# Two-layer decoder with a mixture of experts: the first expert's weight slot handed back in two halves, and the first two experts written out ahead of TensorE's loop

## The chip, the cores and the metric

The kernel runs on one core of a Trainium2 chip, in one launch. The metric is device time in microseconds (us), the median of several runs. Unless it says otherwise, a number with a decimal point below is in us.

## What is computed

A trunk of two layers over 256 tokens of width 1024, all in float32. Layer 0 mixes tokens by a causal convolution module, layer 1 by sparse attention. Each layer then runs a mixture of 32 experts and a gated embedding. The part that matters here, cut down:

```python
def hier_moe(xn, w_rg, b_rg, w_re, b_re, w_gate, w_up, w_down):
    ...                                 # router: top group, then its top 2 experts for each token
    def expert_block(args):
        xblk, e = args
        h = jax.nn.silu(xblk @ w_gate[e]) * (xblk @ w_up[e])    # w_gate, w_up: 1024 x 512
        return h @ w_down[e]                                    # w_down: 512 x 1024
    yb = lax.map(expert_block, (xb, blk_e)).reshape(P, D)
    out = jnp.zeros((N, D), yb.dtype).at[slot_tok].add(yb * slot_w[:, None].astype(yb.dtype))
    return out.reshape(B, T, D)
```

Each token goes to 2 of 32 experts, so an expert sees 16 tokens on average; its three matrices have 2 MB each, 6 MB in all.

## The kernel before, in words

Every engine has a program of its own, and semaphores order them. In both layers all 32 experts are computed, one after the other, each on a slot of 32 tokens. An expert whose tokens don't fit takes extra rounds: they stand in a conditional block ahead of its ordinary code (`pe.If(more > 0)` in `one_expert`, line 671), which holds a second copy of all of the expert's matmuls and is jumped over when there is nothing extra.

**TensorE** (`moe`, `one_expert`). An ordinary expert is, in this order: `gate_up` (line 589), the product of the gathered tokens with gate and up, 32 calls that run over the contraction in 8 steps k = 0 to 7; the gather of the tokens of the expert after it (L580); the transposes of h (L601); the product with down (L608); the transposes of the next tokens (L586); and the scatter into the sums in PSUM (L615). `gate_up` ends with an increment of `gu_mm`, the product with down with one of `y_mm`. The 32 experts are a loop of 16 rounds (line 722) with the code of two experts in it, one for each of the two buffers.

**Weights.** The tile `ring` has two buffers. Each holds gate, up and down of one expert, 48 KB in each of 128 partitions. Even experts use buffer 0 (its three thirds are `R0[0]`, `R0[1]` and `R0[2]`), odd experts buffer 1. The elements of a partition lie in the order of k, so the first 2048 of gate or of up are k = 0 to 3.

**The queue of loads.** All weights are loaded by SyncE's queue (SP), in the order in which its program issues them; a wait in that program holds back all that stands behind it. `expert` (line 320) waits until `gate_up` of the expert two before is done (`gu_mm`), issues gate and up, waits for that expert's product with down (`y_mm`), and issues down. `experts` (line 337) orders a layer: experts 0 and 1 have been loaded before it begins. It first loads the gate of expert 19 in two pieces of 1 MB into tiles that have come free: the first piece into `xnT` once the router's product is done (L345), the second into `h` once ScalarE has copied `h` to the sums (L347, L348). Then comes a loop over pairs of experts from expert 2 on. Parts of experts 16, 17 and 18 are held in other tiles too and are left out of the loop's loads (`held`).

So in the order of the queue: second piece of expert 19's gate; gate and up of expert 2 (wait for `gu_mm` of expert 0); down of expert 2 (wait for `y_mm` of expert 0); gate and up of expert 3 (wait for `gu_mm` of expert 1); and so on.

Of the kernel before, what the change touches and what calls it, by code (L numbers as in the profile page):

```python
# [36 lines left out]
NG, NE, NEG_E = 4, 32, 8  # L37
# [37 lines left out]
def build(nc, x, p, positions, g_mix, g_ffn, g_ple, conv_w_pw1, conv_b_pw1, conv_w_dw, conv_b_dw,  # L75
# [3 lines left out]
    with ExitStack() as ctx:  # L79
# [3 lines left out]
        def sem(name):  # L83
            return ctx.enter_context(nc.semaphore(name))
# [53 lines left out]
        xgT = carve(256).rearrange("p (k s) -> p k s", k=8)  # L138
# [92 lines left out]
        def dense(buf):  # L231
# [3 lines left out]
        R0 = [ring[:, 0, 4096 * i:4096 * (i + 1)] for i in range(3)]  # L235
# [35 lines left out]
        in_in = [sem(f"in_in{i}") for i in range(5)]  # L271
        gu_in = [sem(f"gu_in{i}") for i in range(2)]
        held_in = sem("held_in")
        dn_in = [sem(f"dn_in{i}") for i in range(2)]
        out_st = sem("out_st")
        c_pool, c_dve, c_act = sem("c_pool"), sem("c_dve"), sem("c_act")
# [14 lines left out]
        gu_mm, sil_ok, h_ok, ht_mm, hT_ok, y_mm, y_ok = [  # L291
            sem(s) for s in ("gu_mm", "sil_ok", "h_ok", "ht_mm", "hT_ok", "y_mm", "y_ok")]
# [24 lines left out]
        def _(sp):  # L317
# [20 lines left out]
            def experts(L):  # L338
                def pair(it, held=(None, None)):
                    for s in range(2):  # L340
                        expert(L, it * 2 + s, s, it * 2 + (s - 1 + NE * L), held[s])
                m = HELD // 2
                spare = moe_w_gate[L, HELD + 3].rearrange("(p k) f -> p (k f)", k=8)
                sp.wait_ge(rt_mm, L + 1)
                sp.dma_start(HX[0], spare[:, 0:2048]).then_inc(held_in, 16)  # L345
                sp.wait_ge(hn_dve, HN_AT[3 * L + 1])
                sp.wait_ge(acc_ok, 4 * (L + 1))  # L347
                sp.dma_start(HX[1], spare[:, 2048:4096]).then_inc(held_in, 16)  # L348
                with sp.Fori(1, m) as it:
                    pair(it)  # L350
                pair(m, (0, 1))
                pair(m + 1, (2, 0))
                if L == 0:
                    sp.wait_ge(pp_ok, 4)
                    for i, v in enumerate((nsa_q_norm[0:1, :], nsa_k_norm[0, 1:2, :], nsa_k_norm[0, 2:3, :], nsa_k_norm[0, 0:1, :])):
                        sp.dma_start(gn[:, i, :], v.broadcast_to([P, DH])).then_inc(rot_in, 16)
                    sp.dma_start(invb, inv_freq.broadcast_to([P, DH // 2])).then_inc(rot_in, 16)
                with sp.Fori(m + 2, NE // 2) as it:
                    pair(it)
                for n in range(2):  # L360
                    sp.dma_start(dense(WB[n]), cols(ple_w_gate[L], n)).then_inc(ple_in[n], 16)
# [8 lines left out]
            for i, (c0, c1) in enumerate(PW1_PARTS):  # L370
                for g in range(2):
                    w = conv_w_pw1[0].rearrange("(k p) n -> p k n", p=P)[:, :, D * g + P * c0:D * g + P * c1]
# [68 lines left out]
        def _(pe):  # L441
# [80 lines left out]
            for c in range(KD):  # L522
# [6 lines left out]
                for g in range(2):  # L529
                    w = dense(PW1[2 * (c // 4) + g])  # L530
                    for k in range(KD):
                        xnT_ready(0, k, 1)
                        i = pe.matmul(PS[:, c % 4, g * T:(g + 1) * T], w[:, k, (c % 4) * P:(c % 4 + 1) * P],
                                      xnT[:, k, :], start=(k == 0), stop=(k == KD - 1))
# [51 lines left out]
                    i = pe.transpose(PS[:, BGX, Q4 + P * c:Q4 + P * (c + 1)], xg[:, c::2], ident[:, :])  # L586
                return i

            def gate_up(s, xT):
                for k in range(8):  # L590
                    for j in range(4):
                        w = w_gu(s)[:, j // 2, :, :]
                        i = pe.matmul(PS[32 * j:32 * j + 32, BGU, 0:256].rearrange("q (p c) -> q p c", c=2), xT[:, k, :],  # L593
                                      w[:, k, :].rearrange("q (p h c) -> q h p c", h=2, c=2)[:, j % 2],
                                      start=(k == 0), stop=(k == 7))
                return i

            def h_T():
# [20 lines left out]
            def moe(L):  # L619
# [48 lines left out]
                xg_T().then_inc(xt_mm, 1)  # L668
                rows(W4, 7).then_inc(rt_row, 1)

                def one_expert(it, s):
                    n = it * 2 + (s + NE * L + 1)
                    gi = it * 2 + (s + g0 + 2)
                    ld = it * 16 + 16 * (NE // 2 * L + 1)
                    e = it * 2 + s
                    pe.wait_ge(tab_ok, L + 1)
                    more = pe.value_load(tab[0:1, 0, bass.ds(e, 1)], min_val=0, max_val=7)

                    with pe.If(more > 0):
                        before = pe.value_load(tab[0:1, 1, bass.ds(e, 1)], min_val=0, max_val=64)  # L680
                        pe.wait_ge(xgT_ok, gi - 1)
                        pe.wait_ge(row_act, L + 1)
                        pe.wait_ge(row_dve, L + 1)
                        pe.wait_ge(acc_ok, 4 * (L + 1))
                        pe.sem_inc(pe_step, 1)
                        with pe.Fori(0, more) as r:
                            c = before + r + 1
                            pe.wait_ge(X["x_sel"], c)
                            gather(xsel).then_inc(X["x_ga"], 1)
                            pe.wait_ge(X["x_xg"], c)  # L690
                            xg_T().then_inc(X["x_xt"], 1)
                            pe.wait_ge(X["x_xgT"], c)
                            pe.wait_ge(gu_in[s], ld * 2)
                            gate_up(s, xxgT).then_inc(X["x_gu"], 1)
                            pe.wait_ge(X["x_h"], c)
                            h_T().then_inc(X["x_ht"], 1)
                            pe.wait_ge(X["x_hT"], c)
                            pe.wait_ge(dn_in[s], ld)
                            down(s).then_inc(X["x_y"], 1)
                            pe.wait_ge(X["x_wT"], c)  # L700
                            pe.wait_ge(X["x_ysb"], c)
                            scatter(xwT).then_inc(X["x_done"], 1)

                    pe.wait_ge(gu_in[s], ld * 2)
                    pe.wait_ge(xgT_ok, gi - 1)
                    gate_up(s, xgT).then_inc(gu_mm, 1)
                    pe.wait_ge(sel_ok, it * 2 + (s + (NE + 2) * L + 2))
                    gather(sel[1 - s]).then_inc(ga_mm, 1)
                    pe.wait_ge(row_dve, L + 1)
                    pe.wait_ge(h_ok, n)  # L710
                    h_T().then_inc(ht_mm, 1)
                    pe.wait_ge(row_act, L + 1)
                    pe.wait_ge(dn_in[s], ld)
                    pe.wait_ge(hT_ok, n)
                    down(s).then_inc(y_mm, 1)
                    pe.wait_ge(xg_ok, gi)
                    xg_T().then_inc(xt_mm, 1)
                    pe.wait_ge(wT_ok, gi - 1)
                    pe.wait_ge(y_ok, n)
                    pe.wait_ge(acc_ok, 4 * (L + 1))  # L720
                    scatter(wT[s]).then_inc(wT_free, 1)
                with pe.Fori(0, NE // 2) as it:
                    one_expert(it, 0)
                    one_expert(it, 1)

# [1157 lines left out]
```

## Time and profile before

| | us |
|---|---|
| median of 3 runs (lowest, highest) | 1302.53 (1300.98, 1304.65) |
| the profiled execution, its own time | 1307.97 |
| its span, first to last instruction | 1305.9 |
| TensorE busy in matmuls | 1035.2 (79%) |
| TensorE busy loading weights | 586.6 (45%) |
| VectorE, ScalarE, GpSimd busy | 320.3, 300.4, 456.9 |
| mean granted clock of TensorE | 0.904 of full speed |
| read from HBM | 447.70 MB |

Busy times of different engines overlap. A row of the timeline gives the start, the length, the engine, the line of the code, the operation, the tiles and the count of merged instructions; in brackets stands how long the engine was idle before it and what ended that. "issue" there means that the profile shows nothing that the engine waited for. PEclk is the granted clock of TensorE: 1.00 is 2.4 GHz, 0.50 is 1.2 GHz. L593 is the matmul in `gate_up`; a call of it shows as two matmul records and two weight loads, so one expert's `gate_up` is 64 matmuls. q1 is the queue of the weights, q8 carries instructions, in packets of 16 KB.

### The profile page before, as it was taken

What the parts mean: (1) busy time and instruction counts of PE and PEld (TensorE: products, weight loads), DVE (VectorE), ACT (ScalarE), POOL (GpSimd) and SP (SyncE); (2) the same over time, 40 slices, a digit from 0 to 9 for tenths busy, and PEclk for the clock granted to TensorE, in tenths of its full rate; (3) what the DMA queues carried; (4) which work ended last, traced back from release to release, by engine and by line L of the source; (5) the groups of instructions that cost most, each with busy time, mean ns of one, the idle gap of its engine ahead of it and who ended that gap; (6) DMA issues with size and microseconds to landing.
All of it is one profiled execution on the core that took longest, in us unless ns stands there. A gap on an engine that the chain in (4) does not pass through costs nothing.

```text
span 1305.9 us, 26897 instructions
## 1 busy us (share of the span) xinstructions
PE 1035.2 (79%) x10418; PEld 586.6 (45%) x10419; DVE 320.3 (25%) x890; ACT 300.4 (23%) x708; POOL 456.9 (35%) x743
## 2 busy tenths in 40 slices
PE   6988976676786777679998789887776688678778
PEld 6754543333344434334454555443343345344433
DVE  3994300000021001005126771310000131001111
ACT  5873311111111111112112571211111111112111
POOL 3350263443355334440000130454343464444420
PEclk9999988888899888889999899898888899889989
DMA  9953599999999999999423705699999999999990
GB/s 301 396 192 98 187 411 431 427 430 429 427 430 413 430 430 428 427 422 351 136 65 144 308 5 208 279 404 428 429 429 429 427 429 429 429 428 429 429 410 34
DMA packets 63728, 449.28 MB, mean 344 GB/s; under 512 B 11441, under 2 KB 22313, under 8 KB 38856
## 3 DMA queue, kind: packets, MB, share of 16 engines
q1 hardware_dynamic: 58064, 448.25, 83.0%
q10 hardware_dynamic: 5624, 0.51, 0.3%
q8 instruction: 23, 0.38, 0.1%
q14 instruction: 17, 0.14, 0.0%
HBM read 447.70 MB, written 1.05 MB: 344 GB/s over the span
## 4 chain that ended last, share of the span: by engine, by line
DMA 44%; PE 39%; DVE 9%; ACT 3%; issue 3%; SPq 1%; POOL 1%; ACTq 0%; DVEq 0%
DMA ring<-in_moe_w_up 44%; PE PS L593 15%; PE PS L463 10%; PE PS L570 2%; PE PS L608 2%; ACT arena L1164 1%; PE PS L760 1%; PE PS L615 1%; PE PS L580 1%; DVE arena L1439 1%; PE PS L475 1%; PE PS L451 1%; SPq L322 1%; DVE hn L1439 1%; DVE ppw L1795 1%
## 5 line engine op out<-in xcount | busy, mean ns | idle before, releaser
L593 PE MATMUL PS<-ring,arena 128*32 128x256 f32 x4160 | 335.9, 488 | 181.4 <-DMA ring<-in_moe_w_up 166.3
L593 PEld LDWEIGHTS PS<-ring,arena 128*32 128x32 f32 x4160 | 161.1, 135 | 348.2 <-issue 210.6
L1493 DVE TENSOR_TENSOR arena<-PS,arena 64x256 f32<-64x256 f32 x65 | 27.9, 429 | 580.3 <-ACT arena L1230 575.9
L608 PE MATMUL PS<-ring,arena 128*32 128x256 f32 x2080 | 125.7, 381 | 30.8 <-DVE arena L1496 30.8
L1230 ACT ACTIVATE arena<-PS 64x256 f32<-64x256 f32 x64 | 24.1, 377 | 522.8 <-PE PS L593 522.8
L997 POOL TENSOR_SCALAR arena<-arena 128x32 f32<-128x32 f32 x64 | 18.8, 293 | 289.9 <-PE PS L580 287.3
L956 POOL TENSOR_SCALAR arena<-arena 128x512 f32<-128x512 f32 x67 | 105.6, 1576 | 25.0 <-POOL arena L1003 12.8
L608 PEld LDWEIGHTS PS<-ring,arena 128*32 128x32 f32 x2080 | 73.1, 109 | 61.1 <-issue 37.4
L950 POOL TENSOR_SCALAR arena<-arena 128x32 f32<-128x32 f32 x260 | 88.2, 362 | 13.1 <-POOL arena L997 12.9
L958 POOL TENSOR_TENSOR arena<-arena 128x512 f32<-128x512 f32 x67 | 85.4, 1274 | 5.6
L615 PE MATMUL PS<-arena 32*128 32x256 f32 x1040 | 74.5, 397 | 6.6 <-ACT arena L1228 0.6
L580 PE MATMUL PS<-hn,arena 128*32 128x256 f32 x1072 | 76.6, 394 | 1.6 <-issue 1.6
L1003 POOL TENSOR_SCALAR arena<-arena 128x1 f32<-128x1 f32 x64 | 22.9, 358 | 136.3 <-PE PS L615 136.2
L1488 DVE TENSOR_TENSOR arena<-PS,g 128x256 f32<-128x256 f32 x67 | 28.5, 425 | 170.9 <-PE PS L586 170.9
L463 PE MATMUL PS<-wb,xnT 128*128 128x512 f32 x160 | 70.0, 593 | 0.6 <-DVE xnT L1377 0.6
L1234 ACT COPY arena<-PS 128x256 f32<-128x256 f32 x64 | 23.9, 373 | 162.7 <-PE PS L608 162.7
L615 PEld LDWEIGHTS PS<-arena 32*128 32x128 f32 x1040 | 50.3, 183 | 17.4 <-issue 17.4
L945 POOL TENSOR_TENSOR rstd<-rstd,nhalf 128x1 f32<-128x1 f32 x12 | 7.2, 601 | 130.8 <-DVE rstd L1369 130.8
L960 POOL TENSOR_TENSOR arena<-arena 128x256 f32<-128x256 f32 x67 | 48.9, 731 | 5.2
L580 PEld LDWEIGHTS PS<-hn,arena 128*32 128x32 f32 x1072 | 36.5, 109 | 27.2 <-issue 2.6
L1230 ACT ACT_TABLE_LOAD x32 | 41.1, 1283 | 24.7 <-issue 24.6
L463 PEld LDWEIGHTS PS<-wb,xnT 128*128 128x128 f32 x160 | 30.0, 190 | 36.8 <-issue 36.8
(330 smaller groups left out, 1214.1 us busy)
## 6 DMA issues: line engine op xcount, KB each, us to landing
ring<-in_moe_w_up SPq DMA_DIRECT2D x62, 2048.0 KB, 22.5
ring<-in_moe_w_down SPq DMA_DIRECT2D x62, 2048.0 KB, 24.3
ring<-in_moe_w_gate SPq DMA_DIRECT2D x60, 2048.0 KB, 17.7
wb<-in_ple_w_gate SPq DMA_DIRECT2D x4, 2048.0 KB, 32.4
ring<-in_conv_w_pw SPq DMA_DIRECT2D x3, 2048.0 KB, 18.8
ring<-in_nsa_w_in SPq DMA_DIRECT2D x3, 2048.0 KB, 17.3
wb<-in_moe_w_gate SPq DMA_DIRECT2D x2, 2048.0 KB, 14.9
wb<-in_moe_w_up SPq DMA_DIRECT2D x2, 2048.0 KB, 11.0
```

Source lines behind the costliest of these rows:

```text
L463: i = pe.matmul(PS[:, bank, :], lhs[:, k, t * P:(t + 1) * P], w[:, k, :], start=start and k == 0, stop=(k == KD - 1))
L580: i = pe.matmul(PS[32 * j:32 * j + 32, BGX, 0:Q4].rearrange("q (p c) -> q p c", c=2), lhs[:, t, :], rows[:, j], start=(t == 0), stop=(t == ...
L593: i = pe.matmul(PS[32 * j:32 * j + 32, BGU, 0:256].rearrange("q (p c) -> q p c", c=2), xT[:, k, :], w[:, k, :].rearrange("q (p h c) -> q h ...
L608: i = pe.matmul(PS[32 * j:32 * j + 32, BY, 0:Q4], hT[:, c, 32 * f:32 * f + 32], w_dn(s)[:, f, c, Q4 * j:Q4 * (j + 1)], start=(q == 0), sto ...
L615: i = pe.matmul(PS[:, ACC + j, 256 * t:256 * (t + 1)], w[32 * j:32 * j + 32, t * P:(t + 1) * P], ysb[32 * j:32 * j + 32, :], start=False, ...
L950: i = g.tensor_scalar(eq4[:, t, k, :], c32, S4[:, t, k:k + 1], None, ALU.is_equal)
L956: g.tensor_scalar(eqr, srow, cc, None, ALU.is_equal).then_inc(count, 1)
L958: g.tensor_tensor(eqr, eqr, wrow, ALU.mult).then_inc(count, 1)
L960: g.tensor_tensor(to, eqr[:, 0, :], eqr[:, 1, :], ALU.add).then_inc(ok, 1)
L1230: nc.scalar.activation(gs[64:128, :], PS[0:64, BGU, 0:256], ACT.Silu).then_inc(sil_ok, 1)
L1488: return v.tensor_tensor(dst.rearrange("p (j c) s -> p j c s", c=2), PS[:, BGX, Q4:Q4 + 256].rearrange("p (c j s) -> p j c s", c=2, j=4), ...
L1493: return v.tensor_tensor(hh[64:128, :], PS[64:128, BGU, 0:256], gs[64:128, :], ALU.mult)
```

## The change

SP issues gate and up of expert 2 (the third expert) as four loads of 1 MB in place of two of 2 MB. The first halves (k = 0 to 3) are issued when TensorE has passed the middle of expert 0's `gate_up`, which a new semaphore `gu_half` tells; the second halves when it is done. Down of expert 2 and all of expert 3 follow as before, and the loop over pairs begins one pair later. On TensorE experts 0 and 1 are written out ahead of the loop in each layer, each with its conditional block, since only expert 0 has the increment of `gu_half` in its `gate_up`; the loop has 15 rounds, and ahead of it stands a wait for the first halves (`gu_early`). The programs of the other engines stay as they are.

```diff
+        gu_half, gu_early = sem("gu_half"), sem("gu_early")
...
                 sp.dma_start(HX[1], spare[:, 2048:4096]).then_inc(held_in, 16)
-                with sp.Fori(1, m) as it:
+                wide = [w[L, 2].rearrange("(p k) f -> p (k f)", k=8) for w in (moe_w_gate, moe_w_up)]
+                sp.wait_ge(gu_half, L + 1)
+                for g in range(2):
+                    sp.dma_start(R0[g][:, 0:2048], wide[g][:, 0:2048]).then_inc(gu_early, 16)
+                sp.wait_ge(gu_mm, NE * L + 1)
+                for g in range(2):
+                    sp.dma_start(R0[g][:, 2048:4096], wide[g][:, 2048:4096]).then_inc(gu_in[0], 16)
+                sp.wait_ge(y_mm, NE * L + 1)
+                down_load(L, 2, R0[2], dn_in[0])
+                expert(L, 3, 1, NE * L + 2)
+                with sp.Fori(2, m) as it:
                     pair(it)
...
-            def gate_up(s, xT):
+            def gate_up(s, xT, halves=False):
                 for k in range(8):
...
+                    if halves and k == 3:
+                        i.then_inc(gu_half, 1)
...
-                def one_expert(it, s):
+                def one_expert(it, s, first=False):
...
-                    gate_up(s, xgT).then_inc(gu_mm, 1)
+                    gate_up(s, xgT, halves=first).then_inc(gu_mm, 1)
...
-                with pe.Fori(0, NE // 2) as it:
+                one_expert(0, 0, first=True)
+                one_expert(0, 1)
+                pe.wait_ge(gu_early, 32 * (L + 1))
+                with pe.Fori(1, NE // 2) as it:
                     one_expert(it, 0)
                     one_expert(it, 1)
```

## Rows read from the trace of the kernel before

**Rows 1.** The page: the chain that ended last, and the queue of instructions.

```profile
DMA 44%; PE 39%; DVE 9%; ACT 3%; issue 3%; SPq 1%; POOL 1%; ACTq 0%; DVEq 0%
...
q8 instruction: 23, 0.38, 0.1%
```

**Rows 2.** Windows, layer 0. Columns: stretch, length, engines busy, PEclk, DMA share, GB/s.

```profile
156.00:158.00 2.00, 1.97 (x36) 0.87 (x28) 0.43 (x1) 1.31 (x2) 1.48 (x2) 1.00 0.56 147
...
174.00:176.00 2.00, 1.52 (x24) 0.89 (x22) 0.32 (x2) 0.37 (x1) 1.17 (x4) 1.00 0.97 344
176.00:178.00 2.00, 1.91 (x30) 1.16 (x26) 0.32 (x1) 0.37 (x1) 0.80 (x3) 1.00 1.00 336
178.00:180.00 2.00, 1.36 (x24) 0.77 (x23) 0.11 (x1) 1.28 (x1) 0.69 (x2) 1.00 0.84 328
180.00:588.00 408.00, 296.74 (x3865) 162.81 (x3861) 42.12 (x92) 50.51 (x101) 174.90 (x293) 0.87 1.01 427
```

**Rows 3.** Windows, layer 1.

```profile
852.00:854.00 2.00, 2.00 (x28) 0.95 (x24) 0.00 (x0) 0.00 (x0) 0.00 (x0) 0.62 0.78 320
854.00:856.00 2.00, 1.56 (x16) 0.65 (x8) 0.72 (x2) 0.75 (x2) 0.44 (x2) 1.00 0.64 172
856.00:858.00 2.00, 1.90 (x33) 1.17 (x33) 0.00 (x0) 0.00 (x0) 1.52 (x5) 1.00 0.82 319
858.00:1261.00 403.00, 301.67 (x4009) 168.31 (x4010) 43.69 (x96) 55.86 (x108) 181.51 (x306) 0.88 1.01 429
```

**Rows 4.** Timeline of SP's queue, both layers: DMA issues.

```profile
155.72 0.33 SPq L348 DMA_DIRECT2D h<-in_moe_w_gate  x1
157.26 0.35 SPq L322 DMA_DIRECT2D ring<-in_moe_w_gate  x1
...
173.32 0.33 SPq L322 DMA_DIRECT2D ring<-in_moe_w_gate  x1
...
834.93 0.33 SPq L348 DMA_DIRECT2D h<-in_moe_w_gate  x1
837.41 0.34 SPq L322 DMA_DIRECT2D ring<-in_moe_w_gate  x1
...
854.43 0.33 SPq L322 DMA_DIRECT2D ring<-in_moe_w_gate  x1
```

**Rows 5.** Timeline of TensorE, both layers: the matmuls of gate_up.

```profile
153.22 3.83 PE L593 MATMUL PS<-ring,arena 128*32 128x256 f32 x64 [0.26 <-issue]
...
167.86 5.25 PE L593 MATMUL PS<-ring,arena 128*32 128x256 f32 x64 [5.30 <-issue]
...
179.52 3.84 PE L593 MATMUL PS<-ring,arena 128*32 128x256 f32 x64 [0.64 <-issue]
...
189.49 3.84 PE L593 MATMUL PS<-ring,arena 128*32 128x256 f32 x64 [0.63 <-DMA ring<-in_moe_w_up]
...
832.12 2.45 PE L593 MATMUL PS<-ring,arena 128*32 128x256 f32 x35
835.19 1.79 PE L593 MATMUL PS<-ring,arena 128*32 128x256 f32 x27 [0.62 <-issue]
...
843.05 1.10 PE L593 MATMUL PS<-ring,arena 128*32 128x256 f32 x14 [0.29 <-issue]
848.52 5.47 PE L593 MATMUL PS<-ring,arena 128*32 128x256 f32 x49 [4.37 <-issue]
...
860.36 3.84 PE L593 MATMUL PS<-ring,arena 128*32 128x256 f32 x64 [0.65 <-issue]
```

**Rows 6.** DMA in windows of 0.2 from 165.3, 832.5, 839.5 and 846.1.

```profile
q8 instruction: 1, 0.02, 29.4%
...
q8 instruction: 1, 0.02, 37.6%
...
q8 instruction: 1, 0.02, 30.0%
...
q8 instruction: 1, 0.02, 30.3%
```

## The prediction

> **What bounds the kernel now.** I read the page's chain first: it lies on DMA for 44% of the span and on TensorE for 39% [rows 1]. The windows say where: from 180 to 588 and from 858 to 1261 the queue moves 427 and 429 GB/s and the DMA share is 1.01 [rows 2, 3]. In these 811 us, the two layers' experts, the weights flow without a pause, so only what moves the start of the flow, or makes a pause in it, counts. At 427 GB/s a load of 2 MB takes 4.9 us, an expert 14.7, a piece of 1 MB 2.5.
>
> The queue's timeline then shows what starts the flow. In layer 0 the second piece of expert 19's gate is issued at 155.72 and expert 2's gate at 157.26; in layer 1 at 834.93 and 837.41 [rows 4]. The piece itself gives the queue 2.5 us of work, as much as or more than the 1.54 and 2.48 us between the issues. So the flow starts with the piece, not with expert 2's gate.
>
> The windows show a pause soon after. Piece and expert 2 are 7.3 MB, 17.2 us of flow. Expert 3's gate is issued at 173.32 and 854.43, 17.6 and 19.5 us after the piece [rows 4]; what is lost against 427 GB/s is (83 + 91 + 99) / 427 x 2 = 1.3 us in 174 to 180 of layer 0 [rows 2] and (107 + 255 + 108) / 427 x 2 = 2.2 us in 852 to 858 of layer 1 [rows 3]. With a lag of some 1.3 us from issue to data (an estimate: 19.5 - 17.2 = 2.3 of supply missing, 2.2 seen) a load keeps the flow going when it is issued 1.3 us before the data ahead of it run out.
>
> Expert 3's gate waits for expert 1's `gate_up`, and TensorE's timeline shows why that is late: it stood still for 5.30 us before it in layer 0, and in layer 1 for 4.37 us behind its 14th matmul [rows 5], with nothing that it waited for. What ended these stops is seen in the instruction queue: packets of 16 KB start at 165.3 and 846.1 [rows 6], 2.5 and 2.4 us before TensorE goes on. In layer 1 expert 0 stops too, behind 35 matmuls, for 0.62 us, after a packet at 832.5; a third packet, at 839.5, lies between [rows 6]. From the 35th matmul of one expert to the 14th of the next, two packets' worth of code is passed. An expert has twice 264 matmul and weight-load instructions (ordinary code and the conditional block), some 554 with control; less 42 for the 21 matmuls it is 512, so a packet is 256 instructions. The second round has no such stop: 0.64 and 0.65 us before expert 2 [rows 5], the price of waits and branches. The two loops' 32 rounds and all other code take 23 packets [rows 1], so the loop's code stays once it has come. How long a block takes: at an idle DMA some 3 us (832 to 835.19), under the weights 5.7 (from expert 1's start at 842.8 to 848.52). For the stop in layer 0 I count the program's instructions to the border before it: it lies at the start of expert 0's product with down, some 2.1 us behind `gate_up` (157.05), at 159.2, so up to 8.7 us there. The borders below are counted in the same way. After both long stops `gate_up` runs at half clock: 5.25 in place of 3.84 us [rows 5].
>
> The Trainium skill, Runtime: NRT & Kernel Launch, section Instruction fetch mechanics, says that code comes in blocks of 16 KiB, 256 instructions, and that a taken branch to a block that isn't there forces a fetch first. By that rule, the trace agrees on both. It speaks against new code with jumps in it, and adds no term to the sum.
>
> **The change, part by part.** *First halves earlier: nothing, between -0.9 and 0.* Half of `gate_up` is 1.9 us in, at 155.1 and 834.5, but the halves stand behind the piece in SP's queue, and are issued at 156.1 and 835.3 instead of 157.26 and 837.41. The flow runs then on the piece; and whatever is gained there runs out earlier ahead of expert 3's gate, which still waits for expert 1. The lower bound is the weak start: 147 GB/s in 156 to 158 [rows 2], of which some 0.9 could be filled.
>
> *Smaller loads and SP's issues: nothing, to +0.3.* Two more issues of 0.33 us each [rows 4] and two waits stand ahead of down of expert 2, which is not issued before the product with down is done. That product ends 5 us behind the second halves' release, so it hides them; without that cover they cost 0.7 us.
>
> *The increment and TensorE's new wait: nothing.* The increment rides on a matmul. The wait for the first halves stands where 4.9 us of flow from 157 on are long over (before expert 2 at 179).
>
> *New code, layer 0: 0, between -1.3 and +4.* Each written-out expert has constants for registers, so I take 549 instructions, 5 fewer. Experts 0 and 1 shift by only 5 to 15 instructions, so expert 1's stop stays (if its block comes early, the pause of 1.3 closes). New are the stops of experts 2 and 3, whose code now comes for the first time, under the weights. Expert 2's jump goes into a block asked for at about 174 (in expert 1's gather); at 5.7 to 8.7 us it is there at 180 to 183 instead of 179.5. Its `gate_up` crosses a border near matmul 57: asked for at 181, there at 187, so done near 188. Expert 4's gate may be issued up to 175.9 + 14.7 - 1.3 = 189.3 without a pause (175.9: expert 3's data, 173.32 + 1.3 + the 1.3 lost). Expert 3 then crosses a border near matmul 34, asked for at 194, there at 200, done by 203; the limit for expert 5 is 204.0. What is late next is caught up: an expert costs TensorE about 9.4 us (3.84, and 5.5 for the rest, 157.05 to 162.56) against 14.7 of flow, and at 189.49 it waits for DMA again [rows 5]. At 8.7 us for every block the two `gate_up` end at 191.8 and past 208; I take +4 as the bound, since the one block so slow has three at 5.7 or less beside it.
>
> *New code, layer 1: +2.0, between -2.2 and +5.* Layer 0's two experts put 1098 instructions ahead, four blocks and 74. The border that lay 70 instructions into expert 0's `gate_up` (35 matmuls) now lies at its start, so the 3 us of an unloaded fetch stand bare: `gate_up` goes from 835.1 to 839.0, 1.8 later (3.2 if the clock falls). The second halves, issued then, are in time, since piece and first halves feed the flow to 843.6. The border of expert 1 comes to lie 32 instructions ahead of its `gate_up`, in the code jumped over; that block is asked for when expert 1 begins, at 844.6, and there 5.7 later, 850.3. At half clock `gate_up` ends at 855.7 instead of 854.0. With the half chance of the slower clock before, I take expert 3's gate 2.0 later, and all of that widens the pause. Expert 2 then stops for 3.7 and is done by 871.0, against a limit of 871.1; expert 3 for 2.5, done at 884.5 against 885.8. The bounds are the whole pause closed (-2.2), and 8.7 us for expert 1's block with 1 to 2 for experts 2 and 3 (+5).
>
> **Sum.** 0 + 0 + 0 + 0 + 2.0 = +2.0 on the profiled execution's 1307.97: 1310.0. That execution lies 5.4 above the median of the runs, so for the median 1304.5.
>
> **The rivals.** *Slower:* the blocks come late. The place is expert 2's and 3's first pass and expert 1 in layer 1; it decides once a block takes more than about 7 us under load. For it: the block of 165.3, and a limit that I meet by 0.1 to 1.3 us at four places. Against: the other three blocks. Price: halfway to the bounds, +2.5 in layer 0 and +4 in layer 1, 1309.0.
>
> *Faster by better-lying code:* expert 1's stop shrinks in both layers, both pauses close and the start fills: -1.3 - 2.2 - 0.5 = -4.0, 1298.5. For it: the borders do move. Against: in layer 1 the jump over 285 instructions lands behind a border wherever the count falls within 10 of mine.
>
> *The halves do start the flow earlier*, as if the piece were not there: 157.26 to 156.1 and 837.41 to 835.3, -3.3 with all else kept, 1299.2. Against it stands that the piece fills that time, and that expert 3's gate sets the flow again.
>
> *The change doesn't do what it says:* the halves are issued late, since the piece's wait for ScalarE (L347) holds the queue. Then it is my forecast without any gain to lose.
>
> **Chances.** A measurement of this kernel can tell about 0.3%, 3.9 us, from no change. Forecast, with the last rival in it, 0.56; slower 0.24; better-lying code 0.13; earlier flow 0.07. Within the forecast and the earlier flow, nearly all is within 3.9 us: same 0.62. Slower 0.25, faster 0.13. The range from 1299.0 to 1310.0 reaches nearly to the faster rival and past the slower one's middle; less than 0.1 lies above and some 0.1 below.
>
> **What would show it.** Right: first halves issued about 1 and 2 us ahead of today's gate, with the GB/s after the piece hardly changed; some eight more packets in q8; new stops marked "issue" ahead of or inside `gate_up` of experts 2 and 3; expert 3's gate in layer 1 issued 20.5 to 22.5 us after the piece, and a pause behind it of about 4 us. Wrong: expert 3's gate issued earlier than 17.6 and 19.5 us after the piece; no stops in experts 2 and 3; or gaps in the flow at the loads of experts 4 and 5 in either layer.

## The result, and the profile after

The changed kernel takes 1317.78 us (median of 4 runs, 1315.0 to 1321.01) against 1303.59 for the kernel before in the same comparison: a ratio of 1.0088, 95% interval 1.0067 to 1.0110, so 9 to 14 us slower (the two medians lie 14.2 apart). I had forecast 1304.5 in a range up to 1310.0. The profiled execution has a span of 1313.2.

Of the page, the chain has less DMA and more TensorE and "issue" than in [rows 1], and nine packets of instructions more:

```profile
PE 42%; DMA 39%; DVE 9%; issue 5%; ACT 3%; SPq 1%; POOL 1%; DVEq 0%; ACTq 0%
...
q8 instruction: 32, 0.52, 0.2%
```

The windows of the changed kernel around the loads of experts 3, 4 and 5, first layer 0, then layer 1 (columns as in [rows 2]):

```profile
174.00:180.00 6.00, 5.30 (x76) 3.08 (x68) 1.15 (x3) 1.66 (x4) 2.15 (x7) 1.00 1.02 437
192.00:196.00 4.00, 3.46 (x59) 2.08 (x52) 0.72 (x2) 0.75 (x2) 1.88 (x6) 1.00 0.64 205
208.00:214.00 6.00, 5.52 (x67) 2.90 (x61) 0.72 (x2) 0.75 (x2) 1.72 (x6) 0.74 0.63 216
214.00:560.00 346.00, 254.10 (x3338) 140.80 (x3334) 37.91 (x81) 45.10 (x89) 152.79 (x255) 0.87 1.00 427
...
854.00:860.00 6.00, 5.46 (x74) 3.08 (x70) 0.72 (x2) 0.75 (x2) 1.39 (x5) 0.81 0.44 126
872.00:878.00 6.00, 5.39 (x81) 3.00 (x77) 0.72 (x2) 0.75 (x2) 1.73 (x6) 0.89 0.64 216
890.00:896.00 6.00, 5.45 (x80) 3.05 (x72) 0.72 (x2) 1.12 (x3) 1.97 (x6) 0.97 0.75 281
896.00:1270.00 374.00, 280.19 (x3756) 157.39 (x3760) 41.35 (x90) 51.95 (x100) 170.00 (x286) 0.89 1.01 428
```

Between the pauses and behind them the flow is what it was, 427 and 428 GB/s. The pauses themselves, reckoned as what is missing from 427 GB/s: in layer 0 none ahead of expert 3, then 222 / 427 x 4 = 2.1 and 211 / 427 x 6 = 3.0 us; in layer 1 4.2, 3.0 and 2.1 us. That is 5.1 and 9.3, where [rows 2, 3] gave 1.3 and 2.2. The difference, 10.9 us, is the whole loss within the interval of the result. The span from the issue of the piece of expert 19 in layer 1 to the end of the kernel says the same for layer 1: 1305.9 - 834.93 = 471.0 before, 1313.2 - 835.16 = 478.0 after, 7.1 longer. For layer 0 the spans of these two executions do not bear the windows out: from its piece to that of layer 1 it is 679.2 before and 676.7 after, where the windows give +3.8. One execution can't settle that: the profiled one of the kernel before is a long one (1307.97 against a median of 1303.59), and the kernel with halves only, below, whose pauses are those of the kernel before, has 676.1. So the share of layer 0 rests on the windows.

What makes the pauses is on TensorE. Its timeline, `gate_up` of experts 1, 2 and 3 in layer 0 and 0 to 3 in layer 1 (L593 is L604 now):

```profile
168.00 6.44 PE L604 MATMUL PS<-ring,arena 128*32 128x256 f32 x64 [2.87 <-issue]
...
185.88 6.59 PE L604 MATMUL PS<-ring,arena 128*32 128x256 f32 x61 [5.93 <-issue]
...
201.16 3.46 PE L604 MATMUL PS<-ring,arena 128*32 128x256 f32 x30 [2.97 <-issue]
206.84 3.29 PE L604 MATMUL PS<-ring,arena 128*32 128x256 f32 x33 [2.21 <-issue]
...
835.06 5.20 PE L604 MATMUL PS<-ring,arena 128*32 128x256 f32 x60 [2.29 <-issue]
...
850.94 6.33 PE L604 MATMUL PS<-ring,arena 128*32 128x256 f32 x64 [4.93 <-issue]
...
868.98 5.85 PE L604 MATMUL PS<-ring,arena 128*32 128x256 f32 x64 [6.22 <-issue]
...
885.73 6.01 PE L604 MATMUL PS<-ring,arena 128*32 128x256 f32 x64 [5.19 <-issue]
```

Experts 2 and 3, which in [rows 5] began 0.64 us behind the expert before or waited for DMA, now stop for 5.2 to 6.2 us each, and their `gate_up` takes 5.9 to 7.2 us in place of 3.84, with a granted clock of 0.60 to 0.61 (186 to 192, 869 to 874.5, 886 to 891.5). From one of these `gate_up` to the next it is 17.9 us in layer 0 and 18.0 and 16.8 in layer 1, against 14.7 us of flow for one expert. So SP's queue gets its releases late. Its timeline shows the halves where they were expected, and the gates of experts 4 and 5 where they were not:

```profile
158.46 0.33 SPq L349 DMA_DIRECT2D h<-in_moe_w_gate  x1
158.84 0.44 SPq L353 DMA_DIRECT2D ring<-in_moe_w_gate  x1
...
174.50 0.33 SPq L323 DMA_DIRECT2D ring<-in_moe_w_gate  x1
...
192.90 0.35 SPq L323 DMA_DIRECT2D ring<-in_moe_w_gate  x1
...
210.73 0.33 SPq L323 DMA_DIRECT2D ring<-in_moe_w_gate  x1
```

The first half goes out 0.38 us behind the piece, expert 3's gate 16.0 us behind it, expert 4's 34.4 and expert 5's 52.3. Before it was 17.6 for expert 3 and 27.8 and 37.8 for the other two, which were issued at 183.56 and 193.53.

### The profile page after: what moved, and what is told of

It reads as the page before. It is cut to its first block, busy times and chain, and to the rows that moved or that the text cites. A ratio compares the mean times of both kernels' runs of the same rounds, so it can differ in the third digit from the quotient of the medians.

```text
span 1313.2 us, 26860 instructions
## 1 busy us (share of the span) xinstructions
PE 1035.7 (79%) x10418; PEld 588.2 (45%) x10419; DVE 320.2 (24%) x890; ACT 300.5 (23%) x708; POOL 456.5 (35%) x743
## 4 chain that ended last, share of the span: by engine, by line
PE 42%; DMA 39%; DVE 9%; issue 5%; ACT 3%; SPq 1%; POOL 1%; DVEq 0%; ACTq 0%
DMA ring<-in_moe_w_up 39%; PE PS L604 17%; PE PS L474 9%; PE PS L621 3%; PE PS L581 2%; PE PS L628 2%; PE PS L591 2%; ACT arena L1180 1%; PE PS L776 1%; DVE arena L1455 1%; DVE hn L1455 1%; DVE ppw L1811 1%; PE PS L462 1%; SPq L323 1%; PE PS L597 1%
## 5 line engine op out<-in xcount | busy, mean ns | idle before, releaser
L604 PE MATMUL PS<-ring,arena 128*32 128x256 f32 x4160 | 339.9, 491 | 186.1 <-DMA ring<-in_moe_w_up 149.1
L604 PEld LDWEIGHTS PS<-ring,arena 128*32 128x32 f32 x4160 | 163.9, 136 | 353.8 <-issue 225.4
L1509 DVE TENSOR_TENSOR arena<-PS,arena 64x256 f32<-64x256 f32 x65 | 27.8, 428 | 589.1 <-ACT arena L1246 583.4
L621 PEld LDWEIGHTS PS<-ring,arena 128*32 128x32 f32 x2080 | 73.2, 109 | 61.2 <-issue 37.4
## 6 DMA issues: line engine op xcount, KB each, us to landing
ring<-in_nsa_w_in SPq DMA_DIRECT2D x3, 2048.0 KB, 17.6
```

Of the source, the lines that this page charges most:

```text
L621: i = pe.matmul(PS[32 * j:32 * j + 32, BY, 0:Q4], hT[:, c, 32 * f:32 * f + 32], w_dn(s)[:, f, c, Q4 * j:Q4 * (j + 1)], start=(q == 0), sto ...
L1509: return v.tensor_tensor(hh[64:128, :], PS[64:128, BGU, 0:256], gs[64:128, :], ALU.mult)
```

## The experiments

Theory after the result: only the code written out costs. The first time TensorE runs an expert's code under the flow of weights, it stops 5 to 6 us and then runs `gate_up` at half clock; the halves cost nothing and bring next to nothing. Rivals: the halves themselves cost (smaller loads, a fuller queue); or it is the number of instructions, or entering the loop; or, as my prediction had it, the place of the borders between blocks of code.

### The two parts of the change, each alone

Code written out, loads as before:

```diff
-                with pe.Fori(0, NE // 2) as it:
+                one_expert(0, 0)
+                one_expert(0, 1)
+                with pe.Fori(1, NE // 2) as it:
```

> Experts 0 and 1 written out ahead of TensorE's loop, loads as before (no halves). Theory (the first pass over new code stops TensorE at experts 1, 2 and 3, and the flow of weights pauses ahead of experts 3, 4 and 5): as slow as the changed kernel, ratio to before 1.007 to 1.011; in layer 1 perhaps 1 to 2 us more, since expert 0 starts late and no first halves stand in the queue. Rival (the halves cost the time: smaller loads, or a queue that fills earlier and delays the fetch of code): same as before, within 2 us, and no stop over 1 us in experts 2 and 3.

Halves for expert 2, loop kept (every even expert increments `gu_half`; SP waits for 16 L + 1):

```diff
                 with pe.Fori(0, NE // 2) as it:
                     one_expert(it, 0, first=True)
                     one_expert(it, 1)
+                    pe.wait_ge(gu_early, 32 * (L + 1))
```

> Expert 2's gate and up in halves, TensorE's loop kept whole; the wait for the first halves stands at the end of the loop's round. Every border between blocks of code lies where it lay before. Theory: within 1 us of before, since the piece of expert 19 fills the flow until expert 2's gate and expert 3's gate still waits for expert 1; stops of some 5.3 us (layer 0) and 4.4 us (layer 1) at expert 1 only, pauses in the flow of about 1.3 and 2.2 us. Rival (the halves cost): 5 to 11 us slower. Second rival (the halves bring what they seem to): 2 to 3.5 us faster.

Measured: 1317.17 us written out, ratio 1.0081 (1.0061 to 1.0102), and 1305.90 for the halves, 0.9995 (0.9979 to 1.0011). The windows, first of the kernel written out (two pauses in layer 0, three in layer 1), then of the one with halves only (ahead of expert 3 in each layer):

```profile
190.00:196.00 6.00, 5.25 (x72) 2.70 (x66) 0.72 (x2) 1.07 (x3) 1.97 (x6) 1.00 0.74 262
208.00:214.00 6.00, 5.47 (x72) 2.83 (x64) 0.72 (x2) 0.75 (x2) 1.97 (x6) 0.85 0.49 169
858.00:864.00 6.00, 5.45 (x87) 3.03 (x80) 0.72 (x2) 0.76 (x3) 1.97 (x6) 0.97 0.75 270
876.00:882.00 6.00, 5.33 (x80) 3.00 (x72) 0.82 (x3) 1.12 (x3) 1.97 (x6) 1.00 0.71 257
892.00:898.00 6.00, 5.44 (x84) 3.18 (x76) 0.72 (x2) 0.95 (x3) 1.97 (x6) 0.96 0.83 306
```

```profile
173.00:179.00 6.00, 4.90 (x67) 2.88 (x63) 1.15 (x3) 1.88 (x4) 2.19 (x7) 1.00 0.92 333
850.00:854.00 4.00, 3.46 (x52) 1.90 (x44) 0.72 (x2) 0.75 (x2) 1.97 (x6) 1.00 0.65 209
```

The written-out code alone gives the whole loss, and the halves alone leave the time and both pauses (1.3 and 2.0 us) as they were. The rival that the halves cost falls. The one that they bring 2 to 3.5 us isn't borne out here: the interval goes from 2.7 us faster to 1.4 slower, and no pause is shorter. It comes back below, where no pause follows.

### The suspected cost doubled, and moved to the end

Two rounds written out ahead of the loop (`for it in range(2)`, the loop from 2 on), loads as before:

> Two rounds (experts 0 to 3) written out ahead of the loop, loads as before: the suspected cost doubled. Theory (every expert whose code TensorE runs for the first time under the flow costs its stop of 5 to 6 us and a gate_up at half clock; with the 5.5 us of the rest that makes some 17.3 us against 14.7 us of flow, so each adds a pause of 2 to 3 us): experts 2 to 5 are new in each layer, where the kernel with one round written out has two; 4 experts more in all, 8 to 12 us more than that kernel, 19 to 23 us over before (ratio 1.0145 to 1.0175). Rival (the cost is one of entering the loop, once for each layer): the same time as with one round written out, about 1.008.

The last round written out behind the loop (the loop to `NE // 2 - 1`, then experts 30 and 31), loads as before:

> The last round (experts 30 and 31) written out behind the loop, in place of the first; loads as before. As many instructions as with the first round written out. Theory (a first pass costs where the loads of later experts wait for it): all loads of experts 30 and 31 are in the queue or need only experts 28 and 29, and TensorE waits some 4 us for each expert's weights there, so a stop ahead of expert 30 is half covered; behind the last expert the end of the layer waits for TensorE, so at most one stop's rest and a slow gate_up, 2 to 6 us for each layer: ratio 1.002 to 1.008. The first round as before, pauses of 1.3 and 2.2 us ahead of expert 3 only. Rival (length of code, or the number of packets): 1.008 as with the first round, with pauses ahead of experts 4 and 5.

Two rounds: 1325.52 us, 1.0147 (1.0109 to 1.0184). One round had cost 0.8%, the second costs another 0.7%; a price paid once for entering the loop would have left it at 0.8%. The last round instead of the first: 1313.14 us, 1.0045 (1.0027 to 1.0063), between no cost and that of the first round, with as many instructions. TensorE's timeline of that kernel (L593) at the end of layers 0 and 1 says where the stop counts:

```profile
570.79 5.20 PE L593 MATMUL PS<-ring,arena 128*32 128x256 f32 x64 [3.73 <-DMA ring<-in_moe_w_up]
...
585.52 6.29 PE L593 MATMUL PS<-ring,arena 128*32 128x256 f32 x64 [4.02 <-DMA ring<-in_moe_w_up]
...
1250.71 6.49 PE L593 MATMUL PS<-ring,arena 128*32 128x256 f32 x64 [3.81 <-DMA ring<-in_moe_w_up]
...
1268.10 6.33 PE L593 MATMUL PS<-ring,arena 128*32 128x256 f32 x64 [5.39 <-issue]
```

In layer 0 both of these waits end with the weights, so whatever fetch there was is covered. In layer 1 the last expert stops for 5.39 us, and nothing is left to cover it; in the kernel before it waited 2.79 for its weights, and its `gate_up` took 5.42 for 6.33, so this is 3.5 us.

The first round did not stay as it was, though I had expected that. In layer 1, behind the longer code of layer 0, expert 0 stops for 3.33 us (0.62 before), expert 2's gate goes out 6.1 us behind the piece (836.17 and 842.29; before 2.5), and the flow has a new pause:

```profile
840.00:844.00 4.00, 3.44 (x54) 1.77 (x46) 0.72 (x2) 0.75 (x2) 3.63 (x5) 1.00 0.36 92
```

That is (427 - 92) / 427 x 4 = 3.1 us. With the 3.5 at the end it is 6.6 in the profiled execution, against a measured loss of 5.9 (3.5 to 8.2): less than with the first round, but only half of it lies where I had looked for it.

### Without the jumps

The changed kernel, with the conditional block emitted only inside the loop:

```diff
-                    more = pe.value_load(tab[0:1, 0, bass.ds(e, 1)], min_val=0, max_val=7)
-
-                    with pe.If(more > 0):
...
+                    if not isinstance(it, int):
+                        more = pe.value_load(tab[0:1, 0, bass.ds(e, 1)], min_val=0, max_val=7)
+
+                    if not isinstance(it, int):
+                        with pe.If(more > 0):
...
```

This kernel leaves out the extra rounds of experts 0 and 1, so it is a probe and not a version to use.

> The changed kernel without the conditional blocks (the extra rounds) of the two written-out experts, so their code has no jump and is 268 instructions long instead of 553; extra rounds for experts 0 and 1 are left out. Theory (a jump over the block lands in code that was not asked for in time): expert 1 has no stop in layer 0 and none or under 1.5 us in layer 1; experts 2 and 3 still stop in the loop's first round, but they start 3 to 5 us earlier, so the flow pauses under 1 us in all of layer 0 and under 2 us in layer 1. Time 1 to 4 us below before, that is 12 to 16 us below the changed kernel. Rival (new code costs by its length or by being run for the first time, jump or not): stops at expert 1 of 5 us as before, time near the changed kernel, 8 us or more above before.

The same with expert 2 loaded whole, as before the change:

> Experts 0 and 1 written out without their conditional blocks, expert 2 loaded whole as before: the kernel without blocks less the halves. Extra rounds for experts 0 and 1 are left out. Theory (the piece of expert 19 covers the start, so the halves bring nothing even where expert 3's gate is no longer late): the same as with the halves within 1.5 us, 0.9957 of before. Rival (the halves move the start of the flow by 1 to 2 us in each layer, and it shows once no pause follows): 2 to 3.5 us slower than with the halves, 0.998.

Measured: 1302.45 us, 0.9957 (0.9939 to 0.9975), with the halves, and 1304.12, 0.9981 (0.9964 to 0.9998), without. The first is 5.6 us under before (3.3 to 8.0), more than the 1 to 4 expected. TensorE's timeline of the one with halves, layer 0, `gate_up` of experts 1 to 3 (of the last one the greater part):

```profile
164.82 3.91 PE L604 MATMUL PS<-ring,arena 128*32 128x256 f32 x64
...
180.18 5.42 PE L604 MATMUL PS<-ring,arena 128*32 128x256 f32 x64 [5.97 <-issue]
...
196.82 5.15 PE L604 MATMUL PS<-ring,arena 128*32 128x256 f32 x55 [5.02 <-issue]
```

Expert 1 has no stop at all, though its code too is run for the first time, while experts 2 and 3, which still have their jump, stop for 6.0 and 5.0. So new code alone does not cost; it takes the jump over the block. Two things go out together with the jump. One is the register load ahead of it (`value_load`); but every later round of the loop has it too, and there an expert begins 0.6 to 0.7 us behind the one before. The other is half of the expert's code, 268 instructions for 553, and its length was not varied alone. That the packets simply couldn't keep up with more code does not fit: in the changed kernel one starts at 165.4 and the next at 171.2, and then none until 183.2, while TensorE stands still from 179.95 on. And with experts 0 and 1 some 5 us ahead, the two stops no longer reach the flow: over 170 to 215 it is 427 GB/s, and so it is from 845 to 905 in layer 1.

```profile
170.00:215.00 45.00, 30.56 (x398) 16.46 (x396) 3.54 (x10) 6.00 (x12) 21.18 (x34) 0.85 1.01 427
```

On the halves the rival did better than my theory: I had expected the same time within 1.5 us, the rival 0.998 without halves, and it is 0.9981. The means of the two kernels lie 2.5 us apart. In the first 30 us from the issue of the piece the kernel with halves moves 404 and 404 GB/s, the one without 396 and 400, which is (8 + 4) / 427 x 30 = 0.8 us for both layers; the rest of the difference is not located. The two were timed in different comparisons; a second pair, at the end of this part, was timed in one.

### Moving the borders

The changed kernel with 128 increments of an unused semaphore in the convolution:

```diff
                         pe.matmul(PS[:, 0, :], ident[:, :], xnT[:, 0:2, :].rearrange("p k q -> p (k q)"), start=True, stop=True)
+                    for _ in range(128):
+                        pe.sem_inc(pe_pad, 1)
```

> The changed kernel with 128 increments of an unused semaphore put into TensorE's idle time in the convolution, far ahead of the experts, so that every border between blocks of code moves by half a block in both layers (in layer 0 from 104 and 60 instructions into gate_up of experts 2 and 3 to 24 and 68 ahead of it; in layer 1 to 125, 84 and 36 instructions into the gate_up of experts 0, 1 and 2, where none lay). Theory (the jump over a conditional block costs a whole fetch wherever the border lies): stops of 5 to 6 us in all for each of experts 1, 2 and 3, the same time as the changed kernel within 3 us, ratio 1.0065 to 1.011. Rival (the borders' places decide, as my prediction reckoned): a change of 4 us or more either way, with an expert whose stop is under 2 us or over 9 us.

Measured: 1327.72 us, 1.0162 (1.0131 to 1.0194), outside what the theory allowed. The experiment had a fault that its timeline shows: the increments took the time themselves (first row, the convolution, 14.28 us of "issue" where 3.6 us of waiting had been). The other rows are `gate_up` of experts 1, 2 and 3 in layer 0 and of 1, 2 and 3 in layer 1:

```profile
104.99 3.64 PE L525 MATMUL PS<-arena 128*32 128x256 f32 x32 [14.28 <-issue]
...
181.08 5.78 PE L606 MATMUL PS<-ring,arena 128*32 128x256 f32 x57 [4.84 <-issue]
...
198.53 5.84 PE L606 MATMUL PS<-ring,arena 128*32 128x256 f32 x64 [6.19 <-issue]
...
216.01 5.69 PE L606 MATMUL PS<-ring,arena 128*32 128x256 f32 x64 [6.12 <-issue]
...
860.54 4.42 PE L606 MATMUL PS<-ring,arena 128*32 128x256 f32 x46 [3.10 <-issue]
866.23 1.31 PE L606 MATMUL PS<-ring,arena 128*32 128x256 f32 x17 [1.27 <-issue]
...
875.93 3.05 PE L606 MATMUL PS<-ring,arena 128*32 128x256 f32 x25 [2.68 <-issue]
881.84 3.84 PE L606 MATMUL PS<-ring,arena 128*32 128x256 f32 x36 [2.86 <-issue]
...
897.15 6.13 PE L606 MATMUL PS<-ring,arena 128*32 128x256 f32 x58 [4.82 <-issue]
```

The piece of expert 19 in layer 0 goes out at 167.1 instead of 158.5, and from there to the last down load of the layer it takes 412.5 us against 410.2 in the changed kernel, in layer 1 408.9 against 412.5: 821.4 and 822.7 together. So the time cannot be read as a verdict, but the stops can: the borders moved by half a block, and each of the experts 1 to 3 still stops for 4.4 to 6.2 us in all. Where a border lies inside `gate_up` the stop comes in two parts (2.68 and 2.86), and where it lies elsewhere in one. For experts 1 to 3 the rival had asked for a stop under 2 or over 9 us. Expert 0 is different: in layer 1 it stops for 2.29 us in the changed kernel and not at all here, in layer 0 not at all there and for 1.19 here.

### Going after the pause ahead of expert 3

If expert 3's gate is late, it is expert 3 whose halves should be released early. A first try, loop kept, halves for experts 2 and 3, and TensorE's wait for all four first halves at the end of the round:

```diff
+                    pe.wait_ge(gu_early, 64 * (L + 1))
```

> As the kernel with halves only, but expert 3's gate and up are loaded in halves too, its first halves released in the middle of expert 1's gate_up; loop kept, borders of code as before. Theory (the pause is ahead of expert 3, because expert 1 is late): expert 3's first halves are issued 2.7 us earlier than its gate was, which closes both pauses: 3 to 4 us faster than before (ratio 0.9970 to 0.9977). Rival (pauses come back later, at experts 4 and 5, or smaller loads cost as much as they bring): same as before or slower.

Measured: 1308.72 us, 1.0015 (0.9997 to 1.0033): no gain. The windows ahead of experts 3 and 4 in layer 0 and ahead of expert 4 in layer 1, and `gate_up` of expert 2 in layer 0:

```profile
172.00:178.00 6.00, 5.53 (x82) 3.14 (x78) 0.72 (x2) 0.75 (x2) 2.47 (x7) 0.98 0.99 416
...
190.00:194.00 4.00, 3.44 (x58) 2.06 (x54) 0.72 (x2) 0.75 (x2) 1.69 (x6) 1.00 0.70 242
...
870.00:878.00 8.00, 7.24 (x112) 4.45 (x108) 1.15 (x3) 1.12 (x3) 3.71 (x8) 1.00 0.86 293
```

```profile
185.03 5.83 PE L603 MATMUL PS<-ring,arena 128*32 128x256 f32 x64 [4.67 <-issue]
```

The pause ahead of expert 3 is nearly closed in layer 0 (in layer 1 some 0.8 us are left, 369 GB/s in 852 to 858), but expert 2 now waits 4.67 us for expert 3's halves, and the pause comes back ahead of expert 4. Putting the wait behind expert 1 was the fault. To have no wait of its own, the second try loads gate and up of every expert in halves, so that TensorE's one formula counts four loads for each expert:

> Loop kept whole, but gate and up of every expert are loaded in halves, the first halves released in the middle of the gate_up of the expert two before; so expert 3's first halves go out while expert 1's gate_up still runs, and TensorE has no new wait. Borders of code as before. Theory: the pauses ahead of expert 3 (1.3 and 2.2 us) close, no new ones: 2.5 to 4 us faster than before, ratio 0.997 to 0.998. Rival (loads of 1 MB move less than 427 GB/s, or the many issues on SP come late): the flow of 420 or less, 10 us and more slower. Second rival (the pause moves to expert 4): same as before.

Measured: 1311.18 us, 1.0032 (1.0015 to 1.0049), slower, though the pauses are 0.3 and 1.4 us (407 GB/s in 173 to 179, 329 in 852 to 858). The flow behind them tells why. Two windows of this kernel, then the same two of the kernel before:

```profile
220.00:560.00 340.00, 247.56 (x3191) 135.93 (x3187) 36.35 (x77) 42.32 (x84) 142.85 (x240) 0.86 1.01 423
910.00:1250.00 340.00, 250.06 (x3307) 137.69 (x3308) 37.51 (x80) 47.02 (x90) 152.51 (x256) 0.88 1.01 424
```

```profile
220.00:560.00 340.00, 247.76 (x3200) 135.88 (x3196) 36.38 (x77) 42.33 (x84) 142.84 (x240) 0.86 1.01 427
910.00:1250.00 340.00, 253.51 (x3360) 140.91 (x3364) 37.53 (x80) 46.02 (x89) 150.59 (x254) 0.88 1.01 428
```

1% less flow over 811 us is 8 us lost; the kernel ends up 4.2 slower, so some 4 would be won back, as much as the third try gains by itself. (Only gate and up are split here; down is still loaded whole.) The third try keeps halves for experts 2 and 3 alone and lets each whole load count 32 on the semaphore:

```diff
+                for s in range(2):
+                    expert(L, 2 + s, s, NE * L + s + 1, halves=True)
+                with sp.Fori(2, m) as it:
...
-                    pe.wait_ge(gu_in[s], ld * 2)
+                    pe.wait_ge(gu_in[s], ld * 4)
```

> Loop kept whole; gate and up of experts 2 and 3 alone in halves, each released by the middle of the gate_up of the expert two before; all other loads whole (a whole load counts twice on the semaphore, so TensorE's wait stays one formula and needs no wait of its own). What is computed is all as before. Theory (only the pause ahead of expert 3 is to be had, and 1 MB loads cost only while they run, some 1% of 8 MB of flow in each layer): the pauses of 1.3 and 2.2 us close, the flow stays at 428 GB/s behind: 3 to 4 us faster than before, ratio 0.9970 to 0.9980. Rival (a pause closed ahead of expert 3 comes back ahead of expert 4): same as before, 0.999 to 1.001, with GB/s under 380 in a window of 2 us behind expert 4's gate.

The same with halves for expert 3 alone:

> As the kernel with experts 2 and 3 in halves, but expert 2 whole again: only expert 3's first halves are released early. Theory (expert 2's halves bring nearly nothing, at most the 0.5 us of flow seen at the start): within 1 us of the kernel with both, so 2.5 to 4 us faster than before. Rival (expert 2's halves are worth their 1 to 2 us for each layer): no faster than before.

Measured: 1302.32 us for both in halves, 0.9971 (0.9956 to 0.9987); 1304.11 for expert 3 alone, 0.9989 (0.9971 to 1.0007). Windows of the first, the start of layer 0 and of layer 1:

```profile
160.00:215.00 55.00, 41.77 (x577) 24.42 (x574) 5.01 (x13) 7.44 (x15) 31.47 (x56) 0.94 1.01 427
...
836.00:905.00 69.00, 49.53 (x688) 27.64 (x678) 6.15 (x16) 9.85 (x19) 36.18 (x62) 0.93 1.01 428
```

There is no pause left in either layer, and the flow behind is at 428 (220 to 560). With what the kernel before computes, this is the one version that is faster than both kernels, by 3.8 us (1.7 to 5.7) against before and by some 15 against the changed one. Part of it comes from expert 2's halves, more than I had allowed. That the two ratios' intervals overlap doesn't speak against it, since both are reckoned against the same runs of the kernel before; the two kernels, 12 runs each in one comparison, have means of 1301.96 and 1304.31, 2.35 apart, with an interval of 0.7 to 4.0. The pair without blocks has 2.5. So once no pause follows, the halves of expert 2 are worth some 1 to 4 us for both layers, and expert 3's halves alone are not clearly faster than before. In the first 30 us behind the piece the flow is 402 and 401 GB/s with them and 392 and 398 without, which is 0.9 us; where the rest arises is open.

## Why the prediction was wrong

**Right:** what bounds the kernel, the two pauses and their cause; that the first halves would bring nothing while expert 3's gate waits for expert 1 (in the kernel with halves only they are issued 0.4 us behind the piece in both layers, and the ratio is 0.9995); that the written-out code brings new stops at experts 2 and 3; nine packets where I had said some eight; and one pause to the tenth: ahead of expert 3 in layer 1 I had 2.2 + 2.0, and it is 4.2. The tenth is luck: the gate is issued 22.1 us behind the piece, inside the 20.5 to 22.5 that I had said, but 2.6 later than before and not 2.0. In layer 1 of the changed kernel the first halves were not early at all, 3.0 us behind the piece, since expert 0 stopped as forecast. The direction was forecast (+2.0 us), and "slower" stood among the rivals.

**Wrong:** the size. The term "New code" was mis-sized in both layers: 0 in layer 0, where it is 5.1 - 1.3 = +3.8, and +2.0 in layer 1, where it is 9.3 - 2.2 = +7.1. The step that failed is the one where experts 2 and 3 just met their limits: expert 2 in layer 0 "done near 188" against 189.3, expert 3 "done by 203" against 204.0, in layer 1 "stops for 3.7" and "2.5". Two things in it were off.

First, how much of a fetch is hidden. I let each block be asked for when TensorE crossed the border before it, so that part of its 5.7 us passed beside work. The runs show stops that hardly depend on the border: 5.2 to 6.2 us for experts 2 and 3 in the changed kernel (in layer 1 6.2 and 5.2, where I had 3.7 and 2.5), and 4.4 to 6.2 for experts 1 to 3 with all borders moved by half a block. The block for expert 2 in layer 0, which I had asked for at 174 and there by 183 at the latest, let TensorE go on at 185.88. Its packet of code, and that of expert 2 in layer 1, as the queue of instructions of the changed kernel shows them (DMA in windows of 0.2 from 183.1 and 866.2):

```profile
q8 instruction: 1, 0.02, 34.4%
...
q8 instruction: 1, 0.02, 31.0%
```

They start 3.3 and 3.5 us after TensorE's last matmul ahead of the stop (179.95 and 862.76), and TensorE goes on 2.7 us behind each. For experts 1 and 3 of layer 1 the packets start 2.2 and 2.7 us after the last matmul, at 848.2 and 883.2. So in these four stops the packet itself passed wholly beside idle time. Two stops in layer 0 were ahead of that: expert 1's, 2.87 us, with a packet 0.3 us behind the last matmul, and the first part of expert 3's, 2.97, with one 0.5 behind it. When a block is asked for no trace shows, so why some packets come earlier stays open. The row of 8.7 us that I set aside as one slow block among four was the warning.

Second, and smaller, `gate_up` behind a stop. [rows 5] had 5.25 us for it; for experts 2 and 3 it is 5.9 to 7.2 in the changed kernel. For expert 2 in layer 0 the forecast hardly had it at all: a border near matmul 57 was to end that `gate_up` "near 188" at either clock, since its stop had been made so short.

Together a first pass costs 5.5 us of the rest, 5 to 6 of stop and 6 of `gate_up`, some 17.3 us. Against 14.7 us of flow that is a pause of 2.6 for each; experts 2 and 3 in two layers, 10.4 us. The pauses measured ahead of experts 4 and 5 are 2.1, 3.0, 3.0 and 2.1, 10.2 us. The "slower" rival had the place right; its price of +6.5 was meant to stand halfway to the bounds (halfway is +2 and +3.5, so +5.5), and the bound of layer 1 was too low itself (+5 where it is +7.1; in layer 0 it was +4 where it is +3.8). A margin of 0.1 to 1.3 us at four places in a row, each of which had to hold, should have put the likeliest time on the other side, since every one of them could only be missed in one direction.

**The faster rival** (better-lying code) fell: in layer 0 the pause of 1.3 us did close in the profiled execution (expert 1 stopped 2.87 us for 5.30), but at the price of two others. That the halves start the flow earlier by 3.3 us fell for this kernel with the one that has halves only; its ground, that the piece fills the time, is not the whole of it, since without a pause behind them the same halves bring 0.7 to 4.0 us. One reading was off without effect: the product with down ends 3.8 us behind the release of the second halves (157.05 to 160.88 before), not 5, and covers their issues all the same.

## What to carry to other kernels

Writing the first rounds of a long loop out is not free where the code has jumps like this one, over some 285 instructions: price each first pass as a full fetch stop plus what follows at the lower clock, and compare that sum with the time the bounding transfer gives it, instead of crediting overlap that no row shows. When a load is to be released earlier, look for the transfer ahead of which the flow really pauses, and release that one: here it was the next expert's, and splitting its load too gained where splitting the first alone did not. What comes ahead of the pause shows in the time only once the pause is closed. Split only the loads that need it, and keep the loop whole by letting whole loads count double on the semaphore.

## What the hardware showed that I had not expected

- A jump over some 285 instructions stops TensorE when its target is run for the first time under a full flow: 4.4 to 6.2 us in eleven of the twelve first passes of experts 1 to 3 in the changed kernel and the one with borders moved by half a block, 2.9 in the twelfth. Code without the jump, half as long and run for the first time as well, had no stop (164.82, expert 1). When the fetch is asked for was not found, and no run here varied it alone.
- With gate and up of every expert in loads of 1 MB (rows of 8 KB a partition) the flow is 423 to 424 GB/s, with loads of 2 MB 427 to 428: 1%, and 8 us here.
- 128 semaphore increments in a row held TensorE for up to 14.28 us, at most 0.11 us each.
